# Feed-forward products of 64 rows on alternate halves of TensorE's array, in a two-block transformer kernel

## The reference, cut to what matters

```
# block 1, d_ff = 2816
h = rms_norm(x, ffn_norm)
gate, up = split(h @ w_gate_up)
x = x + (silu(gate) * up) @ w_down          # then a final rms_norm
# block 2, d_ff = 4096, after adaptive modulation by c
h = rmsnorm(x, g_pre_ffn) * (1 + sc2) + sh2
u = relu(h @ w_ff1)
x = x + ga2 * rmsnorm((u * u) @ w_ff2, g_post_ffn)
```

## Time and profile before

| | us |
|---|---|
| median of 3 runs | 749.85 (749.6 to 750.36) |
| profiled execution: span from the first to the last instruction | 747.8 |
| profiled execution: its own time apart from the span | not given by the page |
| TensorE busy | 733.6 |
| VectorE busy | 538.5 |
| ScalarE busy | 377.7 |

### The profile page before, as it was taken

How to read it: one execution, slowest core, us unless ns; L and a number is a source line. 1 busy time by engine, 2 the same in 40 slices (tenths; PEclk the granted TensorE clock), 3 DMA queues, 4 the chain that set the end, 5 groups by cost and what they waited for, 6 DMA issues and landing times.

```text
span 747.8 us, 13134 instructions
## 1 busy us (share of the span) xinstructions
PE 733.6 (98%) x5288; PEld 676.5 (90%) x5288; DVE 538.5 (72%) x927; ACT 377.7 (51%) x544; POOL 51.1 (7%) x72
## 2 busy tenths in 40 slices
PE   7999999999999999999999999999999999999996
PEld 7999987789999999998999999999988998998995
DVE  6798798586677776847669978884967876555554
ACT  7434778664433334446444447665645445445442
POOL 1950000000000000000432000000000000000000
PEclk9999999999999999999999999999999999999999
DMA  8736421478787888642354556554733674644611
GB/s 327 238 121 237 159 66 49 163 305 334 293 319 294 306 322 316 236 163 89 132 196 148 175 201 250 202 187 170 276 118 113 249 258 170 224 168 168 224 57 57
DMA packets 27022, 151.10 MB, mean 202 GB/s; under 512 B 3128, under 2 KB 7836, under 8 KB 9564
## 3 DMA queue, kind: packets, MB, share of 16 engines
q1 hardware_dynamic: 22620, 124.81, 46.0%
q10 hardware_dynamic: 3456, 25.17, 8.5%
q0 software_dynamic: 896, 0.43, 0.3%
HBM read 148.92 MB, written 1.05 MB: 201 GB/s over the span
## 4 chain that ended last, share of the span: by engine, by line
PE 81%; DVE 12%; ACT 3%; DMA 2%; issue 1%; SPq 0%; DVEq 0%; ACTq 0%
PE ps L468 24%; PE ps L469 24%; PE ps L470 24%; DVE ada L1763 4%; DVE w_lo L1667 2%; PE ps L791 2%; DMA raw<-wts 2%; PE ps L589 1%; PE ps L1041 1%; ACT w_hi L1220 1%; DVE w_lo L1740 1%; PE ps L623 1%; PE ps L613 1%; PE ps L641 1%; PE ps L1027 1%
## 5 line engine op out<-in xcount | busy, mean ns | idle before, releaser
L1667 DVE TENSOR_TENSOR w_lo<-raw,w_hi 128x2048 fp32r<-128x2048 f32 (+2 forms) x105 | 237.6, 2268 | 111.9 <-ACT w_hi L1220 111.7
L468 PE MATMUL ps<-h_hi,w_hi 128*128 128x256 f32 (+2 forms) x1000 | 284.7, 285 | 1.1 <-DVE h_lo L1719 1.1
L469 PE MATMUL ps<-h_lo,w_hi 128*128 128x256 f32 (+2 forms) x1000 | 282.8, 283 | 0.0
L470 PE MATMUL ps<-h_hi,w_lo 128*128 128x256 f32 (+2 forms) x1000 | 282.8, 283 | 0.0
L1220 ACT CAST w_hi<-raw 128x2048 fp32r<-128x2048 f32 (+2 forms) x105 | 196.9, 1887 | 50.4 <-PE ps L470 46.5
L468 PEld LDWEIGHTS ps<-h_hi,w_hi 128*128 128x128 f32 (+2 forms) x1000 | 190.2, 190 | 3.4 <-issue 2.3
L469 PEld LDWEIGHTS ps<-h_lo,w_hi 128*128 128x128 f32 (+2 forms) x1000 | 190.3, 190 | 1.2
L470 PEld LDWEIGHTS ps<-h_hi,w_lo 128*128 128x128 f32 (+2 forms) x1000 | 190.2, 190 | 0.3
L468 PE MATMUL ps<-w_hi,mix_hi 128*128 128x512 f32 x248 | 97.4, 393 | 0.4 <-DVE w_lo L1667 0.2
L469 PE MATMUL ps<-w_lo,mix_hi 128*128 128x512 f32 x248 | 96.8, 390 | 0.0
L470 PE MATMUL ps<-w_hi,mix_lo 128*128 128x512 f32 x248 | 96.5, 389 | 0.0
(11 more groups left out here) (313 smaller groups left out, 906.0 us busy)
## 6 DMA issues: line engine op xcount, KB each, us to landing
raw<-wts SPq DMA_DIRECT2D x109, 1024.0 KB, 4.8
ada<-w_ada ACTq DMA_DIRECT2D x24, 1024.0 KB, 5.2
alibi<-wts SPq DMA_DIRECT2D x2, 1024.0 KB, 6.9
fa_whole<-wts SPq DMA_DIRECT2D x2, 1024.0 KB, 6.2
resid<-x SPq DMA_DIRECT2D x2, 512.0 KB, 4.1
raw<-wts SPq DMA_DIRECT2D x2, 512.0 KB, 6.6
rows_ga<-rows_wide SPq DMA_DIRECT2D x1, 1024.0 KB, 6.7
out<-resid SPq DMA_DIRECT2D x4, 256.0 KB, 2.0
```

The lines of the kernel that those rows point to most:

```text
L468: nc.tensor.matmul(o, lh, rh, start=start, stop=False)
L469: nc.tensor.matmul(o, lh, rl, start=False, stop=False)
L470: return nc.tensor.matmul(o, ll, rh, start=False, stop=stop)
L1667: V.tensor_tensor(w_lo[:, s % RING, 0:w], raw[:, n_of[name] % RAW, 0:w], w_hi[:, s % RING, 0:w].bitcast(F32), ALU.subtract).then_inc(w_rea ...
```

## The change

Both kinds of tile are issued as products of 64 rows, alternately on the rows 0 to 63 and 64 to 127 of the array. `feature_rows` takes the place of `feature_tile` in the loops (first loop from step 1, second from step 2): the two halves write into two banks, so a tile is two partial sums. ScalarE copies one of them to SBUF (`keep_part`), VectorE adds the other from PSUM (`add_parts`), and Silu, Relu and the product of gate and up read the sums from SBUF. `half_rows` takes the place of `acc_tile`: in a first phase half 0 of the rows writes output half 0 and half 1 writes output half 1, in a second phase they change banks, so no partial sums are needed; a semaphore (`row_phase`) keeps the phases apart. The banks of the first loop's tiles are now (4, 5) for gate and (6, 7) for up in every step. The last down tiles (`down_half`, `down_part`), the transposes and all other stages keep products of 128 rows.

```
+            def feature_rows(slot, banks):
+                wh, wl = w3(slot, DC)
+                for c in range(2):
+                    for k in range(DC):
+                        for at, (w, h) in enumerate(((wh, h_hi), (wh, h_lo), (wl, h_hi))):
+                            for b in range(2):
+                                rs = slice(b * HD, (b + 1) * HD)
+                                i = nc.tensor.matmul(ps[:, banks[b], c * T:(c + 1) * T], w[rs, k, c * P:(c + 1) * P], h[rs, k, :],
+                                                     start=(k, at) == (0, 0), stop=(k, at) == (DC - 1, 2))
+                return i
+            def acc_phase(slot, hi, lo, m, ph, first):
+                ...
+                for kk in range(2):
+                    for at, (h, w) in enumerate(((hi, wh), (hi, wl), (lo, wh))):
+                        for b in range(2):
+                            n = b ^ ph
+                            rs = slice(b * HD, (b + 1) * HD)
+                            i = nc.tensor.matmul(ps[:, 2 * m + n, :], h[rs, kk, ms], w[rs, kk, n * 512:(n + 1) * 512],
+                                                 start=first and ph == 0 and (kk, at) == (0, 0), stop=False)
+            def half_rows(slot, hi, lo, first, phases):
+                for m in range(2):
+                    acc_phase(slot, hi, lo, m, 0, first).then_inc(row_phase, 1)
+                for m in range(2):
+                    pe.wait_ge(row_phase, phases + m + 1)
+                    i = acc_phase(slot, hi, lo, m, 1, first)
+                return i
...
 # TensorE, ff1_step
-                    if c == 0 and st >= 2:
-                        pe.wait_ge(hid_done, i * 2 + (st - 1))
-                    feature_tile((s0 + c) % RING, ff_bank(st) + c, h_hi, h_lo).then_inc(pe_tile, 1)
+                    if st >= 2:
+                        pe.wait_ge(part_sum, i * 4 + (2 * (st - 2) + c + 1))
+                    feature_rows((s0 + c) % RING, FF1_BANKS[c]).then_inc(pe_tile, 1)
...
 # ScalarE
+            def keep_part(o, bank):
+                nc.scalar.copy(o, ps[:, bank, :]).then_inc(part_kept, 1)
 # ff1_step
-                nc.scalar.activation(ff_act[st % 2], ps[:, ff_bank(st), :], ACT.Silu).then_inc(silu_done, 1)
+                if st:
+                    keep_part(ff_part[0], FF1_BANKS[0][0])
+                    act.wait_ge(part_sum, i * 4 + (2 * (st - 1) + 1))
+                nc.scalar.activation(ff_act[st % 2], ff_sum[0] if st else ps[:, 0, :], ACT.Silu).then_inc(silu_done, 1)
                 after(s0, i)
                 if st >= 1:
+                    act.wait_ge(pe_tile, i * 6 + (s0 + 2))
+                    keep_part(ff_part[1], FF1_BANKS[1][0])
                     after(s0 + 1, i)
 # ff2_step
+                    keep_part(ff_part[0], fa_banks(st)[0])
+                    act.wait_ge(part_sum, i * 3 + (PARTS_1 + st - 1))
 # VectorE
+            def add_parts(o, part, bank, n):
+                dve.wait_ge(part_kept, n)
+                V.tensor_tensor(o, part, ps[:, bank, :], ALU.add).then_inc(part_sum, 1)
 # ff1_step, step 1 and later
-                    after(s0, i)
-                    dve.wait_ge(pe_tile, i * 6 + (s0 + 2))
+                    for c in range(2):
+                        add_parts(ff_sum[c], ff_part[c], FF1_BANKS[c][1], i * 4 + (2 * (st - 1) + c + 1))
+                        if c == 0:
+                            after(s0, i)
+                    dve.wait_ge(part_sum, i * 4 + 2 * st)
...
-                V.tensor_tensor(ff_hid[st % 2], ff_act[st % 2], ps[:, ff_bank(st) + 1, :], ALU.mult).then_inc(hid_done, 1)
+                V.tensor_tensor(ff_hid[st % 2], ff_act[st % 2], ff_sum[1] if st else ps[:, 1, :], ALU.mult).then_inc(hid_done, 1)
 # ff2_step, before the wait for Relu
+                if st >= 2:
+                    add_parts(ff_sum[0], ff_part[0], fa_banks(st)[1], i * 3 + (PARTS_1 + st - 1))
```

More of the change, by code:

```diff
@@ L205, in build @@
         ff_hid = [z[:, 3 + i, :] for i in range(3)]
-        fa_bank = lambda st: 6 + st if st < 2 else 4 + st % 3
+        fa_bank = lambda st: 6 + st
         late_buf = lambda st: 2 if st == FF1_STEPS - 1 else st % 2
@@ L285, in build @@
         s_va = [sem(f"va{i}_landed") for i in range(2)]
+        part_kept, part_sum = sem("row_part_kept"), sem("row_parts_added")
+        row_phase = sem("half_rows_phase")
         rows_first = sem("third_quarter_complete")
@@ L310, in build @@
         va_whole = [alibi[:, i * TW:(i + 1) * TW] for i in range(2)]
-        ff_bank = lambda st: 4 + 2 * (st % 2) if st else 0
+        FF1_BANKS = ((4, 5), (6, 7))
+        fa_banks = lambda st: (4, 5) if st % 3 == 0 else (6, 7)
+        ff_sum, ff_part = ([z[:, a + i, :] for i in range(2)] for a in (10, 12))
+        PARTS_1 = 2 * (FF1_STEPS - 1)
         def tile_width(name):
@@ L518, in acc_tile @@
                         i.then_inc(acc_ps, 1)
+                return i
[10 more added lines that the diff above has]
+            def acc_phase(slot, hi, lo, m, ph, first):
+                wh, wl = w3(slot, 2)
+                ms = slice(m * P, (m + 1) * P)
+                for kk in range(2):
[5 more added lines that the diff above has]
+                                                 start=first and ph == 0 and (kk, at) == (0, 0), stop=False)
+                return i
+            def half_rows(slot, hi, lo, first, phases):
[4 more added lines that the diff above has]
+                    i = acc_phase(slot, hi, lo, m, 1, first)
                 return i
@@ L813, in _ @@
             out_half(3, 1, (1,)).then_inc(pe_tile, 1)
-            def down(slot, buf, first, last):
-                return acc_tile(slot, hid_hi[buf], hid_lo[buf], 0, first, last)
             def ff1_step(st, i=0, first=False):
@@ L822, in ff1_step @@
                     pe.wait_ge(w_ready, i * 6 + (s0 + c + 1))
-                    if c == 0 and st >= 2:
-                        pe.wait_ge(hid_done, i * 2 + (st - 1))
-                    feature_tile((s0 + c) % RING, ff_bank(st) + c, h_hi, h_lo).then_inc(pe_tile, 1)
+                    if st >= 2:
+                        pe.wait_ge(part_sum, i * 4 + (2 * (st - 2) + c + 1))
+                    feature_rows((s0 + c) % RING, FF1_BANKS[c]).then_inc(pe_tile, 1)
                     if (st, c) == (1, 0):
                         pe.wait_ge(hid_done, 1)
-                        turn_hidden(ff_hid[0], 4).then_inc(hid0_turned, 1)
+                        turn_hidden(ff_hid[0], 1).then_inc(hid0_turned, 1)
                 if 1 <= st <= FF1_STEPS - 3:
@@ L831, in ff1_step @@
                     pe.wait_ge(hidlo_done, i * 2 + st)
-                    down((s0 + 2) % RING, (st - 1) % 2, first, False).then_inc(pe_tile, 1)
+                    if st > 1:
+                        pe.wait_ge(pe_tile, i * 6 + (s_idx[f"down{st - 2}"] + 1))
+                    buf = (st - 1) % 2
+                    half_rows((s0 + 2) % RING, hid_hi[buf], hid_lo[buf], first, i * 4 + 2 * (st - 1)).then_inc(pe_tile, 1)
             def ff1_first():
@@ L1124, in ff2_step @@
                 pe.wait_ge(w_ready, i * 6 + (s0 + 1))
-                if st >= 3:
-                    pe.wait_ge(relu2_done, i * 3 + (st - 2))
-                feature_tile(s0 % RING, fa_bank(st), h_hi, h_lo).then_inc(pe_tile, 1)
+                pe.wait_ge(part_sum, i * 3 + (PARTS_1 + st - 2))
+                feature_rows(s0 % RING, fa_banks(st)).then_inc(pe_tile, 1)
                 pe.wait_ge(w_ready, i * 6 + (s0 + 2))
                 pe.wait_ge(hid2lo_done, i * 3 + st)
-                down((s0 + 1) % RING, (st - 1) % 3, False, False).then_inc(pe_tile, 1)
+                pe.wait_ge(pe_tile, i * 6 + (s_idx[f"fb{st - 2}"] + 1))
+                buf = (st - 1) % 3
+                half_rows((s0 + 1) % RING, hid_hi[buf], hid_lo[buf], False, i * 6 + 2 * (FF1_STEPS - 3) + 2 * (st - 2)).then_inc(pe_tile, 1)
             def ff2_first():
@@ L1173, in _ @@
             ff2_step(14)
+            pe.wait_ge(part_sum, PARTS_1 + 13)
             spread(1, 0)
@@ L1176, in _ @@
             pe.wait_ge(w_ready, s + 1)
-            pe.wait_ge(relu2_done, 13)
-            feature_tile(s % RING, fa_bank(15), h_hi, h_lo).then_inc(pe_tile, 1)
+            feature_rows(s % RING, fa_banks(15)).then_inc(pe_tile, 1)
             def down_part(st, m, n):
@@ L1415, in ff1_step @@
                     act.wait_ge(pe_tile, i * 6 + (s0 - 1 + 1))
-                hid = ff_hid[st % 2] if st else ps[:, 4, :]
+                hid = ff_hid[st % 2] if st else ps[:, 1, :]
                 nc.scalar.copy(hid_hi[late_buf(st)], hid.rearrange("p (c t) -> p c t", c=2)).then_inc(hidhi_done, 1)
@@ L1612, in ff2_step @@
                     act.wait_ge(pe_tile, i * 6 + (s_idx[f"fa{st}"] + 1))
+                    keep_part(ff_part[0], fa_banks(st)[0])
+                    act.wait_ge(part_sum, i * 3 + (PARTS_1 + st - 1))
                 if st >= 3:
                     act.wait_ge(hid2_done, i * 3 + (st - 2))
```

(2 more changed lines are left out.)

## The result

| | before | after |
|---|---|---|
| median of 4 runs each, same chip | 749.73 us (749.35 to 750.36) | 758.82 us (757.73 to 759.18) |
| span of the profiled execution | 747.8 us | 755.9 us |
| TensorE busy, products | 733.6 us, 5288 | 736.7 us, 7424 |

The account below looks back on a forecast made before the run. It took TensorE to bound the kernel before, and VectorE with ScalarE the changed first loop: span 747.8 + 3.9 (first part) - 4.8 (second part) = 746.9, plus 2.05 to the median, 749.0 us; range 744 to 758.

Parts of the forecast that it names:

- gap kept: Rival, both loops: each half keeps its gap, pairs 0.120/0.228 us; +4.8 and +1.8, 756.5 us; chance 0.25.
- The pair: TensorE, both loops: a pair of 64-row products takes 0.112 us for 256 columns, about 0.217 for 512.
- the other bound: TensorE, both loops: each half keeps its gap, so a pair takes 0.120 us for 256 columns, 0.228 for 512.
- The 19.1 us: TensorE, both loops: 0.40 us gained on each of 34 first-layer tiles, 0.26 on each of 21 second-layer tiles.
- First part: Up to the second loop: VectorE with ScalarE sets the first loop's step, so this stretch grows by 3.9 us.
- The ring as the bound: First loop: VectorE and ScalarE waiting on each other take 17.64 us a step, where TensorE needs 15.93.
- the second add: First loop, VectorE: adding the second tile's partial sums puts 0.60 plus 0.03 us into each step.
- changes of mode: TensorE, both feed-forward parts: eight switches between 64 and 128 rows at 0.19 us each, 1.5 us in all.
- Second loop: Second part: 0.5 + 5.9 - 0.4 - 1.2 us gained, so -4.8 us.
- The gain of 6.4: Second loop, TensorE: faster pairs gain 0.5 us in the first steps and 5.9 in the nine after.
- 1.2 at the last hidden tile: End of the second loop: copy and add make the last hidden tile's low part later, losing 1.2 us.
- The ring of 11.3: Second loop, steps 2 to 5: VectorE's work with row sums and adds takes 11.3 us a step, TensorE's 10.57.

Follow-up runs that it names:

- e3: Changed kernel with 128-row products everywhere, first-layer tiles still in two banks with the copies and adds: 757.47 us.
- m2: Changed kernel with load_ada issued behind the w_hi cast in the first loop and the last first-layer tile as whole products in one bank: 751.26 us.
- n1: m2 with 128-row products in place of the pairs, first-layer tiles still in two banks with copies and adds: 750.10 us.
- s1: Kernel before with only its 21 second-layer tiles in pairs of 64-row products, first-layer tiles whole, no copies or adds: 758.69 us.
- b1: Kernel before with 14 short series of unused products near the second loop's end, to time single products and pairs; its total time wasn't read.
- p4: Kernel before with four unused copies of 128x512 from PSUM ahead of Silu on ScalarE in each first-loop step: 752.80 us.

## Why the prediction was wrong

The forecast was 749.0 us, the result 758.8; the rival "gap kept", at 756.5, had the right mechanism and was still 2.3 us short.

1. **The pair (failed).** "I take the first, since the pair rows have only 4 to 5 ns over their columns": pairs are 0.120 and 0.227, the other bound. The 19.1 us forecast as gain on TensorE are 0. Two errors lie in it. Each half has to pass its own product every 0.120 us, gap included; both halves have their gap at the same time, so there is nothing behind which to hide it (one half alone and pairs: 3.13 and 3.14 us). And the pairs of the earlier trace rows were plain float32, whose whole products have no gap either; the row "a pair of them is no faster than one full product" pointed to the other bound, and I read it as silent.
2. **First part, +3.9 predicted, +6.25 measured.** The ring as the bound was right, and it was 17.87 us a turn, 17.64 predicted. From sums to w_lo I had 4.45, it was 4.49. The term too small is the second add: 0.63 to the product's start, 0.89 measured (219.97 to 220.86), because the product waits for the end of VectorE's own add. From the sums of step 1 (195.38) to those of step 8 (320.11) it is 124.7 us, 123.3 predicted: 1.4. TensorE was not 0.5 ahead when the loop began, since its pairs gained nothing and its changes of mode cost 0.53: the sums of step 1 end at 195.38, 194.9 predicted, so 0.5, and 1.05 without the 0.57 of the earlier start. Behind the last sums there were 22.9 us to the end of the first token half, 22.5 predicted: 0.4. TensorE waits for w_lo ahead of the gate tiles of steps 5 to 9, 0.6 to 0.9 us each, where 1.7 from step 3 on was predicted: it has no gain to wait out. The three terms make the 2.3 by which the 6.25 exceed the forecast.
3. **Second loop, -4.8 predicted, +1.84 measured.** The gain of 6.4 went with step 1. The rest stands: changes of mode and 1.2 at the last hidden tile (1.23 in the trace). The ring of 11.3 was not needed: TensorE's 11.22 stayed.
4. **Changes of mode.** 1.5 us predicted for eight. The traces have 0.53 for three of them ahead of gate tile 2 and 0.6 for the four of the second part; by times it is 1.35 for eight (e3) and 0.85 for six (m2 and n1). The 0.38 for in and out is what s1's trace shows.
5. **The range.** "Gap kept" gave 4.8 + 1.8, the trace shows 6.25 + 1.84. The range ended at 758, 0.8 below the median; the 1.45 that the rival lacks in the first part are more than that.

## What to carry to other kernels

Splitting a product that fills the array's rows into two half products side by side gained nothing here, neither in fast float32 nor in plain: ask what one half does per product, not what lies idle around a product. A price read from one data type isn't one for another; compare pair and whole of the same kind. Where an engine's idle time ends on another engine that waits for it in turn, go round the ring, add what the change puts in, and compare with the bound: below it costs nothing (two copies, 0.95 of 1.30 us), above it every step pays. And when a ring binds, see first whether a wait in it, here that of two transfers, can be moved out of it.

## What the runs showed of the hardware

- A fast-float32 product of 128 weight columns takes 0.120 us for 256 moved columns, whatever the bank, the weights, the rows (64 or 128) or the sum, and 0.227 for 512, whole or in pairs; with 64 weight columns 0.113 for 256. With 128 moved columns it is no cheaper than about 0.11 us, whole or in pairs (all b1).
- Two loads and two products on the two halves go side by side; in the changed kernel's trace they start 3 to 4 ns apart.
- In and out of the 64-row mode costs 0.38 us of TensorE, with work on both sides (s1).
- Copies of 128x512 from PSUM to SBUF on ScalarE follow each other every 0.477 us, though one alone takes 0.59 (p4). On VectorE the instruction behind one of 128x512 starts 0.60 us after it where it needn't wait for it (220.86 to 221.47); the product that waited for the add right before it started 0.89 after it in the hardware loop (219.97 to 220.86), and 0.71 in steps 8 and 9 outside the loop.
